# Four early expert units instead of three in a fused two-block transformer kernel on one core

## The chip, the core and the metric

One core of one Trainium2 chip runs the whole program. TensorE (PE), VectorE (DVE), ScalarE (ACT), GpSimd (POOL) and SyncE (SP) run their own instruction streams and meet in semaphores; 16 DMA engines move data between HBM and the on-chip memory. The metric is the device time of one execution in microseconds, the median of several. Before the change that is 3735.68 us (3734.17 to 3736.08, 3 runs).

## The reference

Two transformer blocks on 256 tokens of width 2048, all in float32. The first has two layers of attention with grouped and latent heads, the second one layer of attention beside a linear recurrence. The change lies in the last part, a layer of 16,384 experts, of which each token uses 16 in each of 8 heads:

```python
def _peer(h, w_q, k1, k2, u, vt):
    q = (h @ w_q).reshape(B, S, PEER_HEADS, 2, PEER_HALF)
    s1, s2 = (scores of the two halves of q against 128 keys each)
    v1, i1 = lax.top_k(s1, 16)
    v2, i2 = lax.top_k(s2, 16)
    cand = v1[..., :, None] + v2[..., None, :]          # 256 pairs
    vs, ic = lax.top_k(cand, 16)
    e = (index of the pair) = i1 * 128 + i2
    w = jax.nn.softmax(vs, axis=-1)
    act = jax.nn.gelu(einsum('thkd,td->thk', take(u, e), h)) * w
    return einsum('thk,thkd->td', act, take(vt, e))
```

`u` and `vt` are 16,384 x 2048 each, 134 MB.

## The kernel before

The tokens stand in two tiles of 128. A unit is one head of one token tile, so there are 16 units, units 0 to 7 of the first tile and 8 to 15 of the second. For a unit, every token needs 16 rows of `vt`, and 16 dot products of its activations with rows of `u`. A gathered row is one indirect DMA: each of the 128 partitions (tokens) gets its own row of 2048 floats, 1 MB in all.

The kernel gets the dots in two ways. For most units it computes all of them: the dense stage multiplies the activations with the whole of `u`, 128 panels of 1 MB each (512 experts by 4 parts of the contraction), and stores the dots to HBM after every fourth panel (`act_gemm`, L1096 to L1108). Each panel is loaded by SP into one of four buffers, which is free when the remainders of the panel four before are done (L691 to L697). Float32 products are made of three rounded ones: ACT rounds each half panel (`act_half`, L1056), DVE makes the remainder (`dve_half`, L1069), and PE multiplies the halves, 12 matmuls each (`pe_dense`, L856). There are four half panel buffers, and `paced` (L1041) has DVE and ACT issue halves up to two panels ahead of the step that they are in.

Beside it, within the same stage, the first `EARLY` = 3 units are computed in another way: their rows of `u` and then of `vt` are gathered, 32 a unit, and DVE does with each row one instruction, a product summed into a dot for `u` (L1313) or a scaled row added to the sum for `vt` (L1324). After each panel's work, DVE calls `dve_early` with the panel's number `k_`, and ACT `act_early`. A unit has 42 panels: at step 0 its keys are chosen (`choose_keys`, L1584), at step 1 its experts (`choose_experts`, L1591, which ends in the index that POOL waits for), and then the rows follow on four panels of five. There are three row slots (`EARLY_SLOTS`), and POOL gathers row r when DVE is done with row r - 3 (L773 to L784). In the last of the early units the steps without a row also hold the choice of units 3 and 4, the first late ones.

The late stage (`peer`) has the other `LATE` = 16 - `EARLY` = 13 units. POOL gathers for each 16 columns of stored dots and 16 rows of `vt` into 8 slots (L787 to L819); DVE sums 11 of the rows of a unit (L1642) and PE the other five, with the coefficients on a diagonal (L1012). Units from the third late one on are chosen by DVE within this stage, two units ahead (L1632 to L1635). The coefficients of the next unit are made at the end of each unit (L1623). After the eighth unit and at the end the sums are added to `yacc` (L1648, L1649).

In each engine the instructions run in the order of the program; POOL's queue starts with the early rows, and the late gathers wait until all of the dense stage is done on the three engines (L785).

Of the kernel before, what the change touches and what calls it, by code (L numbers as in the profile page):

```python
# [22 lines left out]
ALU = mybir.AluOpType  # L23
# [23 lines left out]
TOPK = 16  # L47


EARLY = 3  # L50
EARLY_STEPS = 2 * TOPK + 10
EARLY_SLOTS = 3
DENSE_SLOTS = 4
PE_ROWS = (2, 5, 8, 11, 14)
# [53 lines left out]
def build(nc, panels, ada, xin, cvec, cols_d, consts_d, bada_d, bf_d, peer_u, peer_v, out):  # L108
    plan = make_plan()
    ctx = ExitStack()  # L110
    with ctx:
# [3 lines left out]
        def sem(name):  # L115
            return ctx.enter_context(nc.semaphore(name))
# [20 lines left out]
        def region(off, *shape):  # L137
            n = int(np.prod(shape))
            v = memh[:, off:off + n] if off < AR else memr[:, off - AR:off - AR + n]
            if len(shape) == 2:  # L140
                v = v.rearrange("p (a b) -> p a b", a=shape[0])
            if len(shape) == 3:
                v = v.rearrange("p (a b c) -> p a b c", a=shape[0], b=shape[1])
            return v
# [38 lines left out]
        def con(name, w):  # L183
            return consts[:, CONSTS[name]:CONSTS[name] + w]
# [380 lines left out]
        hx = region(AR + 8192, D)  # L565
# [12 lines left out]
        yacc = region(B, 2, D)  # L578
# [132 lines left out]
        NSLOT = 8  # L711
        LATE = 2 * HEADS - EARLY
        rows = region(RING, NSLOT, D)
# [7 lines left out]
        early_rows = region(ADAR, EARLY_SLOTS, D)  # L721
# [10 lines left out]
        def small(*shape, dt=F32):  # L732
            v = region(small_at[0], *shape)
            small_at[0] += int(np.prod(shape))
            return v if dt is F32 else v.bitcast(dt)
# [16 lines left out]
        act16 = small(2, TOPK)  # L752
        gel16 = small(TOPK)
        coef = small(TOPK)
# [4 lines left out]
        early_in = [sem(f"early_in{i}") for i in range(EARLY_SLOTS)]  # L759
        early_used = sem("early_used")  # L760
# [3 lines left out]
        def _(pool):  # L764
# [7 lines left out]
            begin(pool, "pool", early_st)  # L772
            for n in range(EARLY):  # L773
                pool.wait_ge(idx_ready, n + 1)
# [12 lines left out]
            def dot(m, j):  # L787

                if j == 0:
                    pool.wait_ge(idx_ready, EARLY + m + 1)  # L790
                    pool.sem_inc(held, 1)
                pool.indirect_dma_start(
                    out=late_act[:, m, j:j + 1], out_offset=None, in_=dots[:, :],
                    in_offset=bass.IndirectOffsetOnAxis(ap=eidx[:, EARLY + m, j:j + 1], axis=0),
                ).then_inc(dots_in[m % 2], 16)

            def row(m, j):

                r = m * TOPK + j
                if r >= NSLOT:  # L800
# [4 lines left out]
                    out=rows[:, r % NSLOT, :], out_offset=None, in_=peer_v[:, :],  # L805
                    in_offset=bass.IndirectOffsetOnAxis(ap=idx[:, EARLY + m, j:j + 1], axis=0),
                ).then_inc(row_in[r % NSLOT], 16)
# [18 lines left out]
        def one_unit(s_, n):  # L826
            if isinstance(n, int):
                return s_[:, n, :]
            return s_[:, bass.ds(n, 1), :].rearrange("p a b -> p (a b)")
# [172 lines left out]
        def pe_peer(pe, st):  # L1002
            for m in range(LATE):
                t, first = (EARLY + m) // HEADS, m in (0, HEADS - EARLY)
                if first and t:
# [265 lines left out]
        def act_wexp(act, n):  # L1271

            act.wait_ge(vs_ready, n + 1)
            act.activation(vexp[:, :], vs[:, :], ACT.Exp, bias=nvs[:, 0:1], accum_out=nvs[:, 1:2]).then_inc(wexp_ready, 1)

        LATE_KEYS = {EARLY_STEPS * (EARLY - 1) + 6: EARLY, EARLY_STEPS * (EARLY - 1) + 16: EARLY + 1}
        LATE_EXPERTS = {EARLY_STEPS * (EARLY - 1) + 11: EARLY, EARLY_STEPS * (EARLY - 1) + 26: EARLY + 1}

        def early_row(step, first):

            a, b = divmod(step - first, 5)
            return 4 * a + b if 0 <= a < TOPK // 4 and b < 4 else None

        def act_early(act, k_):

            n, step = divmod(k_, EARLY_STEPS)
            if n < EARLY and step == 1:
                act_wexp(act, n)
            if k_ in LATE_EXPERTS:
                act_wexp(act, LATE_EXPERTS[k_])  # L1290
            if n < EARLY and step == 21:
                act.wait_ge(early_used, 2 * TOPK * n + TOPK)
                act.activation(gel16[:, :], act16[:, n % 2, :], ACT.Gelu_apprx_tanh).then_inc(gelu_ready, 1)

        def dve_early(dve, k_, chain):

            n, step = divmod(k_, EARLY_STEPS)
            if n >= EARLY:
                return
            if step == 0:  # L1300
                choose_keys(dve, n, chain)
            if step == 1:
                choose_experts(dve, n, chain)
            if k_ in LATE_KEYS:
                choose_keys(dve, LATE_KEYS[k_], chain)
            if k_ in LATE_EXPERTS:
                choose_experts(dve, LATE_EXPERTS[k_], chain)
            j = early_row(step, 2)
            if j is not None:
                r = 2 * TOPK * n + j  # L1310
                dve.wait_ge(early_in[r % EARLY_SLOTS], 16 * (r // EARLY_SLOTS + 1))
                row = early_rows[:, r % EARLY_SLOTS, :]
                dve.tensor_tensor_reduce(row, row, hx, 1.0, 0.0, ALU.mult, ALU.add,  # L1313
                                         act16[:, n % 2, j:j + 1]).then_inc(early_used, 1)
            j = early_row(step, 22)
            if j == 0:
                dve.wait_ge(gelu_ready, n + 1)
                dve.tensor_tensor(coef[:, :], gel16[:, :], wgt[:, n, :], ALU.mult).then_inc(coef_ready, 1)
                dve.wait_ge(coef_ready, n + 1)
            if j is not None:  # L1320
                r = 2 * TOPK * n + TOPK + j
                dve.wait_ge(early_in[r % EARLY_SLOTS], 16 * (r // EARLY_SLOTS + 1))
                dve.wait_ge(early_used, r)
                dve.scalar_tensor_tensor(yacc[:, 0, :], early_rows[:, r % EARLY_SLOTS, :], coef[:, j:j + 1], yacc[:, 0, :],  # L1324
                                         ALU.mult, ALU.add).then_inc(early_used, 1)

        def act_peer(act, st, chain):
# [256 lines left out]
        def choose_keys(dve, n, link):  # L1584

            dve.tensor_copy(tok[:, :], one_unit(tokens, n))
            link(dve.tensor_copy(s12[:, :, :].rearrange("p a b -> p (a b)"), one_unit(scores, n)))
            for a in range(2):
                link(top16(dve, link, s12[:, a, :], s12b[:, a, :], v16[:, a, :], i16[:, a, :]))

        def choose_experts(dve, n, link):  # L1591

            dve.tensor_copy(i16f[:, :, :], i16[:, :, :])
            link(dve.tensor_tensor(cand[:, :].rearrange("p (a b) -> p a b", a=TOPK),
                                   v16[:, 0, :].unsqueeze(2).broadcast_to([P, TOPK, TOPK]),
                                   v16[:, 1, :].unsqueeze(1).broadcast_to([P, TOPK, TOPK]), ALU.add))
            link(top16(dve, link, cand[:, :], candb[:, :], vs[:, :], ic[:, :]))
            dve.tensor_scalar(nvs[:, 0:1], vs[:, 0:1], -1.0, None, ALU.mult).then_inc(vs_ready, 1)
            dve.tensor_scalar(ab[:, 0, :], ic[:, :], 4, None, ALU.logical_shift_right)
            link(dve.tensor_scalar(ab[:, 1, :], ic[:, :], 15, None, ALU.bitwise_and))  # L1600
            link(dve.tensor_copy(abf[:, :, :], ab[:, :, :]))
            for a, buf in ((0, cand), (1, candb)):
                eq = buf[:, :].rearrange("p (k j) -> p k j", k=TOPK)
                link(dve.tensor_tensor(eq, abf[:, a, :].unsqueeze(2).broadcast_to([P, TOPK, TOPK]),
                                       con("iota", TOPK).unsqueeze(1).broadcast_to([P, TOPK, TOPK]), ALU.is_equal))
                link(dve.tensor_tensor(eq, eq, i16f[:, a, :].unsqueeze(1).broadcast_to([P, TOPK, TOPK]), ALU.mult))
                link(dve.reduce_sum(e16[:, a, :], eq, AX_X))
            link(dve.scalar_tensor_tensor(abf[:, 0, :], e16[:, 0, :], float(N_KEYS), e16[:, 1, :], ALU.mult, ALU.add))
            dve.tensor_copy(idx[:, n, :], abf[:, 0, :])
            link(dve.tensor_scalar(abf[:, 1, :], abf[:, 0, :], tok[:, :], None, ALU.add))  # L1610
            dve.tensor_copy(eidx[:, n, :], abf[:, 1, :]).then_inc(idx_ready, 1)
            dve.wait_ge(wexp_ready, n + 1)
            link(dve.reciprocal(nvs[:, 2:3], nvs[:, 1:2]))
            dve.tensor_scalar(wgt[:, n, :], vexp[:, :], nvs[:, 2:3], None, ALU.mult)
# [183 lines left out]
```

## Time and profile before

| | |
|---|---|
| median of 3 runs | 3735.68 us |
| profiled execution | 3738.8 us |
| its span | 3737.1 us |
| mean granted clock of PE | 0.91 |
| busy share of the span: PE, DVE, ACT, POOL | 84%, 67%, 31%, 16% |
| moved by DMA | 915.92 MB, mean 245 GB/s |

Busy times of PE are modelled from pipelined matmuls, so that a matmul of the dense stage has a record of some 390 ns while the next starts before its end. The time of a stage is therefore read from the starts and from the windows, and not from the sum of durations. The share of DMA in a window is the mean busy share of the 16 DMA engines; the granted clock is the part of 2.4 GHz that PE was given.

### The profile page before, as it was taken

The page shows a single profiled execution, that of the slowest core. Times are in us where ns is not written, and L with a number is a line of the kernel's source. Part 1 is how long each engine was busy: PE and PEld are TensorE (multiplying, and loading weights), DVE is VectorE, ACT ScalarE, POOL GpSimd, SP SyncE. Part 2 cuts the span into 40 slices and gives each one's busy share as a digit, 9 for nine tenths or more (in the row PEclk, how much of TensorE's full clock was granted, in tenths as well). Part 3 has the DMA queues.
Part 4 walks back from the last instruction along what each step waited for, and adds up shares of the span by engine and source line. Part 5 has one row for each costly group of instructions (what it writes and reads, how often), then busy time and mean ns, then how long its engine had stood idle before and what let it go on. Part 6 is the DMA issues. An engine that isn't in the chain of part 4 may idle for free.

```text
span 3737.1 us, 39190 instructions
## 1 busy us (share of the span) xinstructions
PE 3130.6 (84%) x14772; PEld 2358.0 (63%) x14772; DVE 2504.1 (67%) x3403; ACT 1153.2 (31%) x1749; POOL 597.4 (16%) x692
## 2 busy tenths in 40 slices
PE   6699998988979989997999689999999984545555
PEld 1488875446758886486997589787887861112222
DVE  4988876746776656455562554777777855778775
ACT  1421225133242343244442443344443430111101
POOL 0000000000100000000000000111111126666662
PEclk9899999989979999898996799999999997777777
DMA  8555760524866763354651234898997968889996
GB/s 350 211 217 226 267 259 1 185 86 181 314 236 249 284 221 124 146 200 168 219 182 38 108 137 175 323 371 309 384 367 309 355 264 302 349 345 361 357 362 262
DMA packets 146983, 915.92 MB, mean 245 GB/s; under 512 B 21617, under 2 KB 30065, under 8 KB 40433
## 3 DMA queue, kind: packets, MB, share of 16 engines
q0 software_dynamic: 75776, 503.47, 35.4%
q1 hardware_dynamic: 56912, 384.82, 26.8%
q10 hardware_dynamic: 14112, 25.17, 1.8%
q8 instruction: 118, 1.93, 0.2%
q14 instruction: 65, 0.52, 0.0%
HBM read 884.03 MB, written 29.36 MB: 244 GB/s over the span
## 4 chain that ended last, share of the span: by engine, by line
PE 60%; DVE 20%; DMA 6%; PEld 5%; issue 4%; ACT 2%; another core or an unknown queue 1%; POOL 0%; DVEq 0%; SPq 0%; ACTq 0%; PEldq 0%; POOLq 0%
PE psum L896 29%; PE psum L869 17%; DVE psum L1642 7%; PEld psum L896 5%; PE psum L973 5%; PE psum L903 5%; DVE junk L1380 2%; PE psum L990 2%; DMA memr<-in_ada_dram 2%; DMA memr<-in_peer_v_dram,memr 2%; DMA memr<-in_panels_dram 1%; PE psum L981 1%; DVE w_lo L1073 1%; PE psum L914 1%
## 5 line engine op out<-in xcount | busy, mean ns | idle before, releaser
L1073 DVE TENSOR_TENSOR w_lo<-memr,w_hi 128x1024 fp32r<-128x1024 f32 x614 | 740.0, 1222 | 457.9 <-ACT w_hi L1067 456.7
L1067 ACT ACTIVATE w_hi<-memr 128x1024 fp32r<-128x1024 f32 x614 | 641.8, 1056 | 954.9 <-PE psum L896 317.4
L1380 DVE CUSTOM_DVE_ANT_0 junk<-memr 128x2048 bf16<-128x2048 f32 x256 | 585.7, 2288 | 126.5 <-DMA memr<-in_ada_dram 85.5
L896 PE MATMUL psum<-h_hi,w_hi 128*128 128x512 f32 (+1 forms) x1696 | 602.4, 355 | 70.0 <-DVE h_lo L1451 47.8
L896 PE MATMUL psum<-h_lo,w_hi 128*128 128x512 f32 (+1 forms) x1696 | 590.3, 348 | 0.0
L896 PE MATMUL psum<-h_hi,w_lo 128*128 128x512 f32 (+1 forms) x1696 | 590.3, 348 | 0.0
L1012 PE MATMUL psum<-memr,memh 128*128 128x512 f32 x520 | 323.3, 780 | 311.3 <-DMA memr<-in_peer_v_dram,memr 198.1
L1012 PEld LDWEIGHTS psum<-memr,memh 128*128 128x128 f32 x520 | 126.0, 254 | 508.2 <-issue 428.6
L869 PE MATMUL psum<-w_hi,l_hi 128*128 128x512 f32 x1024 | 403.5, 394 | 28.6 <-DVE w_lo L1073 28.6
L869 PE MATMUL psum<-w_hi,l_lo 128*128 128x512 f32 x1024 | 402.2, 393 | 0.0
L896 PEld LDWEIGHTS psum<-h_hi,w_hi 128*128 128x128 f32 x1696 | 325.4, 192 | 121.4 <-issue 66.8
L869 PE MATMUL psum<-w_lo,l_hi 128*128 128x512 f32 x1024 | 401.8, 392 | 0.0
L896 PE MATMUL psum<-l_hi,w_hi 128*128 128x256 f32 x1168 | 342.6, 293 | 31.3 <-DVE l_lo L1451 20.9
L771 POOL DMA_DIRECT2D memr<-in_ada_dram x174 | 91.9, 528 | 1717.0 <-DVE mod L1383 1709.7
L1642 DVE SCALAR_TENSOR_TENSOR psum<-memr,memh,psum 128x2048 f32<-128x2048 f32 x141 | 332.0, 2355 | 42.6 <-DMA memr<-in_peer_v_dram,memr 28.0
L896 PEld LDWEIGHTS psum<-h_lo,w_hi 128*128 128x128 f32 x1696 | 326.3, 192 | 41.5 <-issue 3.1
L896 PEld LDWEIGHTS psum<-h_hi,w_lo 128*128 128x128 f32 x1696 | 325.9, 192 | 39.5
L896 PE MATMUL psum<-l_lo,w_hi 128*128 128x256 f32 x1168 | 336.4, 288 | 0.0
L896 PE MATMUL psum<-l_hi,w_lo 128*128 128x256 f32 x1168 | 336.2, 288 | 0.0
L896 PEld LDWEIGHTS psum<-l_hi,w_hi 128*128 128x128 f32 x1168 | 229.8, 197 | 37.4 <-issue 31.8
L869 PEld LDWEIGHTS psum<-w_hi,l_hi 128*128 128x128 f32 x1024 | 194.6, 190 | 72.4 <-DVE w_lo L1073 25.5
L896 PEld LDWEIGHTS psum<-l_lo,w_hi 128*128 128x128 f32 x1168 | 230.7, 198 | 0.4
(182 smaller groups left out, 3816.2 us busy)
## 6 DMA issues: line engine op xcount, KB each, us to landing
memr<-in_panels_dram SPq DMA_DIRECT2D x339, 1024.0 KB, 6.4
memr<-in_ada_dram POOLq DMA_DIRECT2D x176, 1024.0 KB, 5.9
dots<-sq ACTq DMA_DIRECT2D x64, 256.0 KB
memr<-in_xin_dram SPq DMA_DIRECT2D x1, 4096.0 KB, 14.1
gstore<-sq ACTq DMA_DIRECT2D x16, 256.0 KB
memh<-gstore SPq DMA_DIRECT2D x2, 2048.0 KB, 8.0
memr<-gstore SPq DMA_DIRECT2D x2, 2048.0 KB, 10.1
memr<-in_xin_dram SPq DMA_DIRECT2D x2, 2048.0 KB, 7.3
```

Source lines behind the costliest of these rows:

```text
L771: pool.dma_start(adar[:, s_, :], ada[i * 2 + s_]).then_inc(ada_in[s_], 16)
L869: ins = pe.matmul(bank(2 * (group % 2) + t), x_[:, kc, t * P:t * P + P], u_[:, c, :], start=kc == 0 and j == 0, stop=kc == DC - 1 and j == 2)
L896: ins = pe.matmul(bank(o["bank"])[:, 0:o["w"]], w_[:, c, :], x_[:, kc, :], start=kc == 0 and j == 0, stop=kc == DC - 1 and j == 2)
L903: ins = pe.matmul(bank(o["bank"])[:, a:b], lt, rh, start=j == 0, stop=j == len(pairs) - 1)
L914: pe.matmul(bank(4 + gr["ms"] % 2)[:, 0:w], ones[:, :], sq[:, n % 2, 0:w], start=j == 0, stop=j == len(gr["x"]) - 1).then_inc(sq_used, 1)
L973: ins = pe.matmul(o, lt, rh, start=j == 0, stop=j == len(mms) - 1, skip_group_check="forget" in u)
L990: ins = pe.matmul(bank(O_BANK + u["hn"] % 2)[:, u["col"]:u["col"] + P], u["v"][c], probT[:, u["n"] % 2, c * P:c * P + P], start=c == 0, st ...
L1012: ins = pe.matmul(bank(b), diags[:, q % DIAGS, :], rows[:, r % NSLOT, 512 * b:512 * b + 512], start=first and i == 0, stop=(EARLY + m) % H ...
L1067: act.activation(w_hi[:, m % HALVES, :, :], slot[:, 8 * i:8 * i + 8, :], ACT.Copy).then_inc(hi_ready, 1)
L1073: dve.tensor_tensor(w_lo[:, m % HALVES, :, :], raw_panel(o["g"])[0][:, 8 * i:8 * i + 8, :], w_hi[:, m % HALVES, :, :].bitcast(F32), ALU.su ...
L1380: chain(dve.tensor_tensor_reduce(junk[:, :], w, cact[:, v_, :], 1.0, 0.0, ALU.mult, ALU.add, mod[:, a, m:m + 1]))
L1642: dve.scalar_tensor_tensor(sums_dve, row, by, sums_dve, ALU.mult, ALU.add).then_inc(row_added, 1)
```

## The change

`EARLY` goes from 3 to 4, and the steps of an early unit from 42 to 32, so that the four units take the 128 panels exactly. Every panel now has a row: step j handles row j of `u` for j < 16 and row j - 16 of `vt` after. Keys and experts of unit 0 are chosen together at the first panel; those of unit n + 1 are chosen at steps 8 and 20 of unit n, beside its rows. The second late unit is chosen at panels 118 and 124. The gelu of a unit moves from step 21 to step 15, and its coefficients to step 16. `LATE` becomes 12, by its definition.

```diff
-EARLY = 3
-EARLY_STEPS = 2 * TOPK + 10
+EARLY = 4
+EARLY_STEPS = 2 * TOPK
...
-        LATE_KEYS = {EARLY_STEPS * (EARLY - 1) + 6: EARLY, EARLY_STEPS * (EARLY - 1) + 16: EARLY + 1}
-        LATE_EXPERTS = {EARLY_STEPS * (EARLY - 1) + 11: EARLY, EARLY_STEPS * (EARLY - 1) + 26: EARLY + 1}
-
-        def early_row(step, first):
-
-            a, b = divmod(step - first, 5)
-            return 4 * a + b if 0 <= a < TOPK // 4 and b < 4 else None
+        KEYS_AT = {EARLY_STEPS * n + 8: n + 1 for n in range(EARLY)}
+        EXPERTS_AT = {EARLY_STEPS * n + 20: n + 1 for n in range(EARLY)}
+        KEYS_AT[EARLY_STEPS * EARLY - 10], EXPERTS_AT[EARLY_STEPS * EARLY - 4] = EARLY + 1, EARLY + 1
...
-            if n < EARLY and step == 1:
-                act_wexp(act, n)
-            if k_ in LATE_EXPERTS:
-                act_wexp(act, LATE_EXPERTS[k_])
-            if n < EARLY and step == 21:
+            if k_ == 0:
+                act_wexp(act, 0)
+            if k_ in EXPERTS_AT:
+                act_wexp(act, EXPERTS_AT[k_])
+            if step == TOPK - 1:
                 act.wait_ge(early_used, 2 * TOPK * n + TOPK)
                 act.activation(gel16[:, :], act16[:, n % 2, :], ACT.Gelu_apprx_tanh).then_inc(gelu_ready, 1)
...
-            if step == 0:
-                choose_keys(dve, n, chain)
-            if step == 1:
-                choose_experts(dve, n, chain)
...
+            if k_ == 0:
+                choose_keys(dve, 0, chain)
+                choose_experts(dve, 0, chain)
+            if k_ in KEYS_AT:
+                choose_keys(dve, KEYS_AT[k_], chain)
+            if k_ in EXPERTS_AT:
+                choose_experts(dve, EXPERTS_AT[k_], chain)
+            r = 2 * TOPK * n + step
+            row = early_rows[:, r % EARLY_SLOTS, :]
+            if step == TOPK:
                 dve.wait_ge(gelu_ready, n + 1)
                 dve.tensor_tensor(coef[:, :], gel16[:, :], wgt[:, n, :], ALU.mult).then_inc(coef_ready, 1)
                 dve.wait_ge(coef_ready, n + 1)
...
+            dve.wait_ge(early_in[r % EARLY_SLOTS], 16 * (r // EARLY_SLOTS + 1))
+            if step < TOPK:
+                dve.tensor_tensor_reduce(row, row, hx, 1.0, 0.0, ALU.mult, ALU.add,
+                                         act16[:, n % 2, step:step + 1]).then_inc(early_used, 1)
+            else:
+                j = step - TOPK
                 dve.wait_ge(early_used, r)
-                dve.scalar_tensor_tensor(yacc[:, 0, :], early_rows[:, r % EARLY_SLOTS, :], coef[:, j:j + 1], yacc[:, 0, :],
+                dve.scalar_tensor_tensor(yacc[:, 0, :], row, coef[:, j:j + 1], yacc[:, 0, :],
                                          ALU.mult, ALU.add).then_inc(early_used, 1)
```

## Rows read from the trace of the kernel before

**Rows 1.** Windows by stretch: us, busy (count) of PE, PEld, DVE, ACT, POOL; clock; DMA share; GB/s.
```profile
2334.00:3068.00 734.00, 708.49 (x3072) 582.83 (x3072) 567.75 (x624) 307.63 (x336) 111.17 (x96) 0.98 0.87 339
...
3104.00:3347.50 243.50, 126.11 (x200) 49.27 (x200) 184.69 (x282) 26.59 (x56) 153.89 (x164) 0.76 0.87 333
3347.50:3702.00 354.50, 197.22 (x320) 76.71 (x320) 268.06 (x360) 29.01 (x65) 214.47 (x227) 0.77 0.92 364
```

**Rows 2.** The same view, an undisturbed piece of the dense stage.
```profile
2380.00:2560.00 180.00, 180.00 (x796) 149.10 (x795) 137.20 (x108) 79.33 (x84) 28.32 (x26) 1.00 0.96 374
```

**Rows 3.** Timeline of DVE, two row steps: start us, us, instruction.
```profile
2402.18 2.29 DVE L1313 CUSTOM_DVE_ANT_0 memr<-memr 128x2048 f32<-128x2048 f32 x1
...
2407.62 2.29 DVE L1313 CUSTOM_DVE_ANT_0 memr<-memr 128x2048 f32<-128x2048 f32 x1
```

**Rows 4.** Chain of waits in the dense stage: start us, us, what.
```profile
2370.12 209.26 PE psum L869 x912
...
2608.44 206.81 PE psum L869 x900
...
2847.42 40.87 PE psum L869 x168
```

**Rows 5.** Windows at the second unit start and at a late choice of experts.
```profile
2590.00:2620.00 30.00, 22.98 (x90) 18.11 (x89) 22.49 (x37) 9.92 (x13) 6.67 (x6) 0.89 0.82 320
...
2890.00:2920.00 30.00, 29.63 (x131) 24.21 (x130) 28.28 (x49) 13.89 (x17) 5.00 (x4) 1.00 0.89 341
```

**Rows 6.** Timeline of DVE in the late stage: the coefficients of four units.
```profile
3143.16 0.17 DVE L1623 TENSOR_TENSOR memh<-memh,memr 128x16 f32<-128x16 f32 x1
3195.54 0.17 DVE L1623 TENSOR_TENSOR memh<-memh,memr 128x16 f32<-128x16 f32 x1
...
3623.75 0.17 DVE L1623 TENSOR_TENSOR memh<-memh,memr 128x16 f32<-128x16 f32 x1
3662.20 0.17 DVE L1623 TENSOR_TENSOR memh<-memh,memr 128x16 f32<-128x16 f32 x1
```

**Rows 7.** Timeline of DVE at the first unit start.
```profile
2343.44 0.15 DVE L1586 COPY memr<-consts 128x1 f32<-128x1 f32 x1
...
2348.13 2.36 DVE L1073 TENSOR_TENSOR w_lo<-memr,w_hi 128x1024 fp32r<-128x1024 f32 x2
...
2357.62 0.17 DVE L1611 CAST memr<-memr 128x16 uint32<-128x16 f32 x1
...
2357.90 0.23 DVE L1614 TENSOR_SCALAR memr<-memr 128x16 f32<-128x16 f32 x1
...
2366.63 2.29 DVE L1313 CUSTOM_DVE_ANT_0 memr<-memr 128x2048 f32<-128x2048 f32 x1 [6.24 <-DMA memr<-in_peer_u_dram,memr]
```

**Rows 8.** DMA issues of the last 1737 us, with KB each and us to landing.
```profile
memr<-in_panels_dram SPq DMA_DIRECT2D x160, 1024.0 KB, 5.0
dots<-sq ACTq DMA_DIRECT2D x64, 256.0 KB
```

**Rows 9.** Windows in which the DMA engines were busy all the time or nearly.
```profile
2840.00:2870.00 30.00, 25.03 (x100) 20.12 (x99) 23.51 (x36) 9.95 (x12) 4.57 (x4) 0.89 1.00 410
2990.00:3020.00 30.00, 30.00 (x134) 24.84 (x133) 25.47 (x18) 12.65 (x13) 9.09 (x5) 1.00 1.01 409
3650.00:3680.00 30.00, 18.39 (x30) 7.00 (x28) 19.09 (x10) 1.78 (x6) 13.70 (x15) 0.77 1.01 419
2600.00:2700.00 100.00, 94.88 (x408) 77.99 (x407) 75.17 (x66) 39.98 (x42) 16.13 (x16) 0.97 0.98 384
```

**Rows 10.** The early gathers on POOL (L781): issue duration ns min/median/max, and landing.
```profile
L781 POOL DMA_INDIRECT memr<-in_peer_u_dram,memr x48: 932/1140/1577, 2358.8 to 2929.3; - x48
...
DMA to landing us min/median/max: 5.6/9.8/12.8
```

**Rows 11.** The page's group of ACT's roundings: busy, mean ns, idle before.
```profile
L1067 ACT ACTIVATE w_hi<-memr 128x1024 fp32r<-128x1024 f32 x614 | 641.8, 1056 | 954.9 <-PE psum L896 317.4
```

**Rows 12.** Waits in the dense stage: engine line waited for: us in total, times, longest.
```profile
DVE memr L1313 <- DMA memr<-in_peer_u_dram,memr: 18.7, 3, 6.3
```

## What the change was forecast to do, worked out from these rows

> **What bounds the kernel now.** I read the stretches first [rows 1]: dense dots 2334 to 3068 us, a fill, the sums of late units 3104 to 3702 us, and an end of 35 us. Dense and late stretch have different limits, and that is the whole question, since the change carries work from the second to the first.
>
> In the dense stretch 3072 matmuls (128 panels of 24) keep PE busy; an undisturbed piece has 796 of them in 180 us [rows 2], so 24 x 180 / 796 = 5.43, and the row steps of DVE come 5.44 us apart [rows 3]. 128 x 5.44 = 696 us, while the window that holds all 3072 is 734.0 long [rows 1], some 3 us of it at its edges (the matmuls end at about 3066.5): 34 us are lost. The chain of waits shows where [rows 4]: PE runs undisturbed from 2370.1 to 2579.4 and from 2608.4 to 2815.3; at each of the three unit starts DVE chooses a unit and then stands for its first gathered row [the first in rows 7], and PE runs dry behind it. The second start has 7.0 us of PE idle in 30 and a granted clock of 0.89, so part ran at 1.2 and not 2.4 GHz [rows 5]. From 2370.12 to 2608.44 are 84 half panels, 228.5 us of work in 238.3: one such start costs 9.8 us, the next (to 2847.42) 10.5.
>
> In the late stretch DMA is what is short: share 0.87 and 0.92, PE busy about half, DVE about three quarters [rows 1]. The coefficients of consecutive units stand at 3143.16 and, ten units later, 3623.75 [rows 6]: 48.06 us a unit for 16 rows.
>
> **The change, part by part. Base:** the profiled execution took 3738.8 us (span 3737.1); the runs' median is 3735.68, 3.1 less. Differences are worked out in the profile and set on the median.
>
> (1) A late unit goes: 13 to 12. Units 4 and 5 are now chosen beforehand, as 3 and 4 were, and the last two need no choice either, so the missing one is a middle one, with its choice: **-48.1 us**. Bounds: the last units' spacing of 38.5 (3623.75 to 3662.20) and the first's 52.4. The fill and the end stay.
>
> (2) Two unit starts in the dense stage go, units 1 and 2, since each choice now comes while the unit before is still being gathered: -9.8 - 10.5 = **-20.3**. The row that was late there is then asked for as any other row is. What is late next is (4) and (5).
>
> (3) The first start gets worse. Now four half panels of DVE work stand between keys, experts and the first row; after the change none do. The choice ran from 2343.44 to 2358.1 with one pair of remainders (2.3) from 2348.13 on in it [rows 7]: keys 4.7, experts 7.7. Without the pair it ends at 2355.8; the row is there 8.8 us after its index (2357.8 to 2366.6), which now stands at 2355.5, so 2364.3, its product ends 2366.6 and the next half panel's remainder 2367.8. PE starts half 5 then, where before it started half 9 at 2370.12. Four halves are 10.9 us, less 2.2 gained: **+8.7**. Bounds 5 and 12, by when the first four rows come. The one slow-clock piece stays.
>
> (4) Choices beside rows. In steady work DVE finishes a half panel 2.3 us after PE frees its buffer (ACT's rounding 1.06 [rows 11], the remainder 1.2), and PE isn't out of halves until 4 x 2.72 = 10.9 us after. With a row (2.3) and the next remainder (1.2) DVE is done at 5.8: 5.1 us of cover. Keys (4.7) fit. Experts (7.7) miss by 2.6, in four places. Before, a late choice of experts stood on a step without a row, with 5.1 + 2.3 = 7.4 us of cover, and cost 0.37 us of PE (29.63 busy of 30 [rows 5]) where this reckoning gives 0.3. DVE then catches up at 5.44 - 2.3 - 2.35 = 0.8 us a panel, enough for the 12 to 20 panels to the next choice. The last pair (experts at 116, keys 118, experts 124) doesn't get that time: about 3 us each. Sum 4 x 2.6 + 6 - 0.7 = +15.7. The gelu after row 15 makes ACT wait for DVE's product and load a table, some 2.7 us, inside the cover. Bounds: 0 if panels are late anyway, +13 more if each stall costs slow clock as a start does.
>
> (5) Bytes. A panel and a row are 1.049 MB each, the dots stored 0.131 MB a panel [rows 8]. Before, 4 of 5 panels had a row: 10.09 MB in 27.2 us = 371 GB/s wanted, and 374 at a share of 0.96 was moved [rows 2]. After: 2.228 MB in 5.44 us = 410 GB/s wanted. What can be had? Thirty-microsecond pieces at a share of 1.00 or 1.01 moved 410 and 409 GB/s in this stage and 419 in the late one; 100 us at 0.98 moved 384, so 392 full [rows 9]. I take 397: 5.61 us a panel, 0.17 over PE's, x 118 panels = +20. DMA thus becomes the limit, barely. It works on while DVE chooses (up to three rows and four panels are on order), so of (4) only some 4 us come on top: (4) and (5) together **+24**. Bounds: 16 (410 holds, PE's own rate), and 60 at 377 GB/s.
>
> Total bytes give much the same: when the first row is issued (2356.5) 122 panels, 128 rows and 16.8 MB of dots are left, 278.9 MB / 397 = 702 us, to 3059; in the last four panels nothing but rows is left to load, 9 us unused, and five choices let the queues run thin by 1 or 2 us each: end at about 3077 against 3066.5, +11. The parts give -20.3 + 8.7 + 24 = +12.4.
>
> (6) Rows 126 and 127 are now summed beside the last panels, DVE done before PE's last half and the last dots are stored; +1 for that tail (0 to 5).
>
> Sum: -48.1 + 12.4 + 1 = -34.7, rounded -35: **3701 us** (3704 for a profiled execution).
>
> Where page and trace differ: a full share gives 392 to 419 GB/s here [rows 9]. The Trainium skill, DMA: Bandwidth & Descriptors, "Where 436 GB/s comes from", says of HBM to SBUF that the HBM side binds, at about 358; an estimate by that page is 285.2 MB (278.9 and the six panels before) / 358 = 797 us of dense stage, 66 more than now, and a total some 18 us slower. The trace speaks against it in this run. The same skill's HBM Reference, "Specifications", names it the share when both cores of a pair stream, and about 425 for one alone.
>
> **Rivals.**
>
> A, DMA keeps up at 410 and (5) is nothing: dense -20.3 + 8.7 + 15.7 = +4, total -43: 3693. For it: 409 and 410 over 30 us. Against: 392 full over 100 us.
>
> B, each wait costs more than itself: DVE has 4.65 of 5.6 us filled, and a late row holds up the next remainders and so PE, with the clock behind it. Say 384 GB/s, the best 100 us [rows 9]: 5.80 us, +0.36 x 118 = 42, and 4: dense +34, total -13: 3723. For it: the tight coupling of one DVE stream with both gates. Against: now DVE waits for a row three times only, 18.7 us in all, the three starts [rows 12].
>
> C, slower: three row slots are too few once there is no panel without a row. A slot's round is the sum (2.35), 0.3 until POOL has it, the issue 1.14 and the landing, shared by three: with the median landing of 9.8 us [rows 10] 4.5 us a row, with the longest, 12.8, 5.5. The spare panels that let the slots refill are gone. With a landing of 15 us a row takes 6.26: 0.82 x 118 = 97, dense +85, total +38: 3774. It costs more than it saves from 5.91 us a panel on (118 x 0.47 = 56, with 4 the 60 above), a landing of 13.9 us. For it: landings must grow as the share stays at 1. Against: growth stops when the rows on order fall. By the Trainium skill (DMA: Bandwidth & Descriptors, "Queues, rings and completion order") each DMA engine takes turns between queues that have work; by that, panels couldn't starve the rows. No row shows the sharing itself.
>
> D, the memory side gives no more over a whole stage than the 364 GB/s that the long late piece moved [rows 1]: (278.9 + 6.3) MB / 364 = 784 us, +53 in dense, total +5: 3741. Against: that piece had a share of 0.92, so it wasn't full. By the page's 358, above, this is what would happen.
>
> **How the numbers follow.** Forecast 0.49, A 0.20, B 0.18, C 0.10, D 0.03. A measurement of this kernel tells 0.2% (7.5 us) from no change. Faster: forecast and A, and four fifths of B, 0.83; same 0.06, from B's slow end and the mild end of C; slower 0.11. Range for 8 in 10: from 3680 (A with (3) and (4) near their low ends) to 3738 (377 to 384 GB/s).
>
> **What would show it.** Dense stage: DMA share at 1.00 in nearly all windows, 392 to 405 GB/s, 5.6 us between row steps, matmuls ending about 741 us after their start; one start stall of some 18 us and no others of that kind; DVE waits for rows in the middle of units. Late stage: 12 x 16 rows, the same 48 us a unit, the same 36 us fill. Wrong if DMA's share there stays at 0.97 with panels at 5.44 (A), if row landings pass 13 us with the share under 0.95 (C), or if late units take other than 45 to 50 us.

## The result and the profile after

The changed kernel takes 3704.12 us (3702.0 to 3706.42, 4 runs) against 3735.88 for the kernel before beside it; ratio 0.991, 95% interval 0.9891 to 0.9928. The forecast was 3701, faster. The total came out as forecast; two of its terms, (4) and (5), did not, and nearly cancelled, so that the total is right in part by luck.

The changed kernel's windows, as in [rows 1]: dense stage, then the late units of the first and of the second tile.

```profile
2342.00:3087.00 745.00, 714.16 (x3070) 586.43 (x3071) 647.34 (x716) 308.64 (x338) 141.90 (x128) 0.97 0.93 378
...
3122.00:3316.00 194.00, 97.69 (x160) 38.36 (x160) 144.41 (x226) 20.54 (x43) 122.50 (x131) 0.77 0.86 327
3316.00:3670.00 354.00, 198.58 (x320) 76.88 (x320) 272.14 (x361) 31.82 (x71) 217.69 (x231) 0.79 0.94 370
```

Where each stage begins and ends is read best from the first and last start of one instruction: PE's third product of the dense stage (L869), the coefficients of a late unit (L1613) and the closing sums (L1638). Durations are min/median/max in ns, then the starts in us.

```profile
L869 PE MATMUL psum<-w_lo,l_hi x1024: 387/389/628, 2344.3 to 3087.4; 128*128 128x512 f32 x171
...
L1613 DVE TENSOR_TENSOR memh<-memh,memr x12: 168/169/231, 3125.3 to 3626.4; 128x16 f32<-128x16 f32 x12
...
L1638 DVE TENSOR_TENSOR memh<-psum,memh x2: 2291/2292/2292, 3315.9 to 3670.5; 128x2048 f32<-128x2048 f32 x2
```

The same three instructions in the kernel before:

```profile
L869 PE MATMUL psum<-w_lo,l_hi x1024: 387/389/628, 2336.8 to 3066.0; 128*128 128x512 f32 x171
...
L1623 DVE TENSOR_TENSOR memh<-memh,memr x13: 167/168/176, 3103.8 to 3662.2; 128x16 f32<-128x16 f32 x13
...
L1648 DVE TENSOR_TENSOR memh<-psum,memh x2: 2291/2292/2292, 3342.9 to 3702.1; 128x2048 f32<-128x2048 f32 x2
```

So, in the two profiled executions (spans 3737.1 and 3704.5):

| | before | after | |
|---|---|---|---|
| up to the dense stage | 2336.8 | 2344.3 | +7.5 |
| dense matmuls | 729.2 | 743.1 | +13.9 |
| fill | 37.8 | 37.9 | +0.1 |
| late units | 598.3 (13) | 545.2 (12) | -53.1 |
| end | 35.0 | 34.0 | -1.0 |
| span | | | -32.6 |

The first line is no work of the change: nothing ahead of the dense stage differs, and over the twelve profiles of this study that start lies anywhere from 2332.7 to 2354.8 (three of them clear the sums later, which is worth 3.5).

The line of the late units holds something that the change didn't do, too. The unit that goes is one of the first token tile. Up to the first closing sums that tile's late units took 239.1 us before (3103.8 to 3342.9) and 190.6 after (3125.3 to 3315.9): 48.5 less. The other 4.6 us came in the eight units of the second tile, on which nothing was changed: 359.2 before, 354.6 after, and 360.9 when the changed kernel ran again (e0).

Windows of 30 us in the changed kernel's dense stage: two that PE fills, and two with a choice of experts in them.

```profile
2740.00:2770.00 30.00, 30.00 (x134) 24.86 (x133) 24.30 (x22) 13.63 (x15) 6.44 (x6) 1.00 1.01 406
2800.00:2830.00 30.00, 30.00 (x134) 24.86 (x133) 26.12 (x22) 14.04 (x15) 6.63 (x6) 1.00 1.02 425
...
2470.00:2500.00 30.00, 26.98 (x113) 21.88 (x112) 28.26 (x41) 11.90 (x15) 6.16 (x5) 0.94 0.91 361
3010.00:3040.00 30.00, 26.98 (x106) 21.71 (x106) 27.46 (x56) 11.50 (x15) 4.63 (x4) 0.89 0.87 355
```

DMA moves up to 425 GB/s with a row on every panel, and PE has no idle there: it isn't held to 397. The time goes in the other windows, 3.0 us of PE idle each. The chain of waits has PE's pieces behind the first start and behind four of the five choices of experts, and the timeline of PE has its wait at the first of these choices.

```profile
2372.91 46.51 PE psum L869 x192
...
2488.04 97.04 PE psum L869 x420
...
2667.40 97.14 PE psum L869 x420
...
2846.97 98.40 PE psum L869 x420
...
3027.97 33.11 PE psum L869 x132
```

```profile
2488.04 0.80 PE L869 MATMUL psum<-w_hi,l_hi 128*128 128x512 f32 x1 [3.02 <-DVE w_lo L1073]
```

192 matmuls are 16 half panels, 43.5 us of work, and took 3.0 more. 420 are 35 halves, 95.2 us, and took 1.8, 1.9 and 3.2 more; 132 are 11 halves, 29.9 us, and took 3.2 more: the slow clock behind the idle time (granted 0.94 in the window of the first choice, 0.89 in that of the fourth). PE's idle time was 3.0 to 3.1 us at each of the five; behind the fifth, three halves before the end of the stage, 1.9 more went to the slow clock. A choice of experts thus costs 4.8 to 6.3 us.

Waits of the changed kernel in the dense stage (us in total, times, longest; 6.5 us of the first line lie ahead of the stage's first matmul):

```profile
PE psum L869 <- DVE w_lo L1073: 35.8, 8, 13.5
...
DVE memr L1309 <- DMA memr<-in_peer_u_dram,memr: 17.0, 13, 6.2
...
DVE memh L1314 <- DMA memr<-in_peer_v_dram,memr: 4.3, 8, 1.0
```

DVE now waits for rows in the middle of units, 21 times instead of 3 [rows 12], but for 21.3 us in all, 6.2 of them at the start.

### The profile page after: what moved, and what is told of

Same layout as the page of the kernel before. It is cut to its first block, busy times and chain, and to the rows that moved or that the text cites. A ratio compares the mean times of both kernels' runs of the same rounds, so it can differ in the third digit from the quotient of the medians.

```text
span 3704.5 us, 39156 instructions
## 1 busy us (share of the span) xinstructions
PE 3104.6 (84%) x14732; PEld 2344.8 (63%) x14732; DVE 2548.1 (69%) x3440; ACT 1150.6 (31%) x1744; POOL 597.9 (16%) x692
## 4 chain that ended last, share of the span: by engine, by line
PE 58%; DVE 19%; DMA 7%; issue 5%; PEld 5%; POOL 3%; ACT 2%; another core or an unknown queue 1%; DVEq 0%; ACTq 0%; SPq 0%; PEldq 0%; POOLq 0%
PE psum L896 28%; PE psum L869 15%; PEld psum L896 5%; DVE psum L1632 5%; PE psum L973 5%; PE psum L903 5%; DMA memr<-in_ada_dram 3%; DVE junk L1370 3%; PE psum L990 2%; DVE w_lo L1073 2%; DMA memr<-in_peer_v_dram,memr 1%; POOL memr L804 1%; PE psum L981 1%; POOL memh L792 1%; DMA memr<-in_panels_dram 1%
## 5 line engine op out<-in xcount | busy, mean ns | idle before, releaser
L1012 PE MATMUL psum<-memr,memh 128*128 128x512 f32 x480 | 296.3, 776 | 285.4 <-DMA memr<-in_peer_v_dram,memr 181.1
L869 PE MATMUL psum<-w_hi,l_hi 128*128 128x512 f32 x1024 | 406.6, 397 | 36.0 <-DVE w_lo L1073 35.8
L1012 PEld LDWEIGHTS psum<-memr,memh 128*128 128x128 f32 x480 | 115.2, 252 | 466.0 <-issue 423.1
L869 PE MATMUL psum<-w_hi,l_lo 128*128 128x512 f32 x1024 | 404.3, 395 | 0.0
L869 PE MATMUL psum<-w_lo,l_hi 128*128 128x512 f32 x1024 | 403.7, 394 | 0.0
L1632 DVE SCALAR_TENSOR_TENSOR psum<-memr,memh,psum 128x2048 f32<-128x2048 f32 x130 | 306.1, 2355 | 62.7 <-DMA memr<-in_peer_v_dram,memr 37.9
L869 PEld LDWEIGHTS psum<-w_hi,l_hi 128*128 128x128 f32 x1024 | 195.8, 191 | 81.5 <-DVE w_lo L1073 33.9
```

Of the source, the lines that this page charges most:

```text
L869: ins = pe.matmul(bank(2 * (group % 2) + t), x_[:, kc, t * P:t * P + P], u_[:, c, :], start=kc == 0 and j == 0, stop=kc == DC - 1 and j == 2)
L1012: ins = pe.matmul(bank(b), diags[:, q % DIAGS, :], rows[:, r % NSLOT, 512 * b:512 * b + 512], start=first and i == 0, stop=(EARLY + m) % H ...
L1632: dve.scalar_tensor_tensor(sums_dve, row, by, sums_dve, ALU.mult, ALU.add).then_inc(row_added, 1)
```

## The experiments

Three groups of kernels ran, each beside its own runs of the kernel before: e1, e2, e3 and e5; then e0, e4 and e6; then e7, e8 and e9. The medians of the kernel before were 3685.67, 3747.0 and 3739.35 us. Totals are therefore differences of medians within a group; the ratios are worked out from all runs and need not be those of the medians. Stage times are from one profiled execution each, dense matmuls as in the table above.

| kernel | total against before, ratio (95%) | dense | late (units) |
|---|---|---|---|
| e1, overlap alone | -23.4, 0.9936 (0.992 to 0.9953) | 710.4 | 537.5 (13) |
| e2, cut choices | -55.5, 0.9852 (0.9836 to 0.9869) | 718.3 | 494.5 (12) |
| e3, two slots | +57.6, 1.0154 (1.0134 to 1.0174) | 838.9 | 494.4 (12) |
| e5, soft start | -72.5, 0.9802 (0.9786 to 0.9818) | 704.7 | 492.2 (12) |
| e0, the change again | -34.0, 0.9903 (0.9871 to 0.9935) | 743.1 | 545.9 (12) |
| e4, five early | +8.9, 1.0016 (0.9995 to 1.0037) | 840.0 | 503.2 (11) |
| e6, e5 with half panels | -88.3, 0.9751 (0.9713 to 0.9789) | 700.4 | 547.5 (12) |
| e8, the change with half panels | -30.7, 0.9919 (0.9887 to 0.995) | 742.7 | 548.5 (12) |
| e7, e4 with half panels | -44.4, 0.9878 (0.9842 to 0.9915) | 780.2 | 494.8 (11) |
| e9, e5 again | -77.5, 0.9795 (0.9756 to 0.9833) | 706.7 | 548.1 (12) |

**Overlap alone (e1).** Three early units with the rows where they were; the choices of units 1 and 2 move to rowless panels of the unit before. Against the kernel before (panel: unit; both pieces of a choice of experts stand on one panel, so that it isn't cut):

```diff
-            if step == 0:
-                choose_keys(dve, n, chain)
-            if step == 1:
-                choose_experts(dve, n, chain)
...
+        KEYS_AT = {0: 0, 26: 1, 68: 2, 90: 3, 100: 4}
+        PICK_AT = {1: 0, 31: 1, 73: 2, 95: 3, 110: 4}
+        EXPERTS_AT = {1: 0, 31: 1, 73: 2, 95: 3, 110: 4}
```

> One part of the change alone: still three early units on 126 panels and a row on four panels of five, but units 1 and 2 are chosen on rowless panels while the unit before is summed. Theory 1 (step 2 of the forecast: a unit start costs 10 us of the dense stage because its first row is asked for too late): dense matmuls take 730.6 - 20 = 710 us, the late stage stays at 598, total 3716 us. Rival (the starts cost nothing of their own, the lost time is DVE work that has to be done anyway): 730 us and 3736.

Dense 710.4 us:

```profile
L868 PE MATMUL psum<-w_lo,l_hi x1024: 388/389/632, 2334.9 to 3045.3; 128*128 128x512 f32 x171
```

18.8 less than in the profile before, and 23.4 of the total (20 expected). The profile before belongs to another group, but dense stages repeat across groups: 743.1 twice for the changed kernel, 704.7 and 706.7 for e5 and e9. Step (2) stands: a start cost the wait for its row, and that is gone when the row is asked for early.

**Cut choices (e2).** `choose_experts` becomes `pick_pairs` (to the 16 best pairs) and `name_experts` (the rest), on different panels. The keys move too, and the last choices move apart.

```diff
-        KEYS_AT = {EARLY_STEPS * n + 8: n + 1 for n in range(EARLY)}
-        EXPERTS_AT = {EARLY_STEPS * n + 20: n + 1 for n in range(EARLY)}
...
+        KEYS_AT = {0: 0, 4: 1, 36: 2, 68: 3, 98: 4, 113: 5}
+        PICK_AT = {0: 0, 11: 1, 43: 2, 75: 3, 103: 4, 118: 5}
+        EXPERTS_AT = {0: 0, 19: 1, 51: 2, 83: 3, 108: 4, 123: 5}
```

> The changed kernel, with the choice of experts cut in two (the top 16 pairs, 3.5 us; the naming of the experts, 4.2 us) on panels some seven apart, so that no piece of choosing is over the 5.1 us of cover. Theory 1 (DMA can carry 410 GB/s; what the changed kernel loses in the dense stage are five stalls of PE behind an uncut choice of 7.7 us, some 3 us of idle and 1.8 us of slow clock each): dense matmuls 744 - 24 = 720 us, total 3680 us. Theory 2 (step 5 of the forecast: DMA's 397 GB/s sets 5.61 us a panel whatever DVE does): at least 738 us, total 3698 or more.

Windows of e2: the whole stage, and two of 30 us at the places where the changed kernel had a choice of experts.

```profile
2341.00:3060.00 719.00, 703.25 (x3072) 578.97 (x3070) 644.10 (x715) 309.27 (x338) 148.02 (x128) 0.99 0.96 391
2470.00:2500.00 30.00, 30.00 (x133) 24.54 (x132) 29.02 (x32) 14.90 (x19) 5.89 (x5) 1.00 1.01 402
2650.00:2680.00 30.00, 30.00 (x134) 24.86 (x133) 28.80 (x20) 12.74 (x14) 7.31 (x6) 1.00 1.00 398
```

718.3 us, 24.8 under the changed kernel, with the same bytes and the same DVE work. Theory 1 holds to 2 us, and in the total as well (-55.5, where 3680 meant -56); theory 2 would have kept the stage over 738. The cover of 5.1 us, worked out in step (4), the time that DVE can be away beside a row before PE runs dry, is the size that matters: behind the start, PE waits three times in this stage, 0.5, 1.1 and 0.4 us, where it waited 3.0 to 3.1 five times. How much the new places of the last choices add to the cut isn't separated; the first four uncut choices had 12 panels without a choice before them, and cost PE as much idle time as the fifth.

**Two row slots (e3).** `EARLY_SLOTS = 2` in the changed kernel.

> The changed kernel with two row slots instead of three. Rival C's reckoning, a slot's round shared by the slots: (2.35 + 0.3 + 1.14 + 9.8) / 2 = 6.8 us a row with the landing of before, dense 870 to 890 us, total 3840; if the landing falls to some 7.8 us with fewer rows on order, 5.8 us a row, dense 762 us, total 3722. If slots don't matter at all: 3704.

```profile
L869 PE MATMUL psum<-w_lo,l_hi x1024: 387/389/632, 2335.0 to 3173.9; 128*128 128x512 f32 x171
...
DMA to landing us min/median/max: 5.7/9.1/12.5
```

```profile
DVE memr L1309 <- DMA memr<-in_peer_u_dram,memr: 98.1, 54, 6.4
DVE memh L1314 <- DMA memr<-in_peer_v_dram,memr: 70.4, 45, 5.8
```

Rival C's round gives (2.35 + 0.3 + 1.14 + 9.1) / 2 = 6.45 us a row with the landing measured, 825 us for 128 rows; 838.9 were measured. That is 2% off, with a landing known only afterwards. The stage is 31 to 51 us shorter than the 870 to 890 that I expected, since the landing came down from 9.8 to 9.1 (0.35 us a row, 45 us); the total of 3840 meant +104, and +57.6 came. C's mechanism is real, DVE waiting 168 us for rows in 99 waits; three slots are just clear of it: in e2 the median landing is 11.9 us and the round (3.8 + 11.9) / 3 = 5.2, under the 5.44 of a panel.

**Soft start (e5, and again as e9).** On top of e2: first choice in three pieces on panels 0, 1 and 2, clearing on panel 3, row r on panel r + 4, and four panels with two rows.

```diff
+        KEYS_AT = {0: 0, 12: 1, 40: 2, 66: 3, 92: 4, 108: 5}
+        PICK_AT = {1: 0, 21: 1, 47: 2, 73: 3, 98: 4, 115: 5}
+        EXPERTS_AT = {2: 0, 28: 1, 54: 2, 79: 3, 104: 4, 121: 5}
+        ROWS_AT = lambda k_: tuple(range(k_ - 4 + sum(k_ > d for d in (34, 61, 87, 126)), k_ - 3 + sum(k_ >= d for d in (34, 61, 87, 126)))) if k_ >= 4 else ()
...
+            if k_ == 3:
+                chain(dve.memset(yacc, 0.0))
...
-            if st.get("early"):
-                chain(dve.memset(yacc, 0.0))
```

> The kernel with the cut choices, and a start in which DVE makes its remainders between the pieces of the first choice, clears the sums on panel 3 instead of ahead of the stage, and takes the first row on panel 4; the four rows that are then behind are taken as a second row on panels 34, 61, 87 and 126. Theory 1: the start's 19 us (16 idle, 3 slow clock) fall to under 4, and 3.5 us of clearing go from ahead of the first matmul: dense matmuls 705 us, total 3662 us. Rival (two rows on one panel, or the end of the stage with two rows to sum, give it back): 3672 or more.

704.7 us, as expected (705). Within the stage PE waits 1.3 us at the longest, where it waited 13.5, and 3.5 us ahead of its first matmul, where that was 6.5.

```profile
2340.00:3045.00 705.00, 699.54 (x3071) 575.22 (x3071) 644.95 (x716) 311.11 (x340) 149.14 (x128) 1.00 0.98 401
3104.00:3500.00 396.00, 231.70 (x377) 89.67 (x376) 351.42 (x534) 46.23 (x99) 292.49 (x310) 0.81 1.01 403
```

> The kernel with the cut choices and the soft start once more, beside others of this group, to see whether its 72.5 us hold where the kernel before is slower than it was beside it the first time. The dense stage gives 730.6 - 704.7 + 3.5 = 29 us on any chip; a late unit fewer gave between 43 and 53 us. So 72 to 82 us, ratio 0.978 to 0.981.

-77.5 us and 0.9795, as expected, dense 706.7. It is the best kernel of the study.

```profile
3104.00:3500.00 396.00, 211.53 (x331) 82.22 (x332) 309.31 (x461) 41.08 (x87) 256.86 (x272) 0.78 0.91 356
```

This last row is e9's late stage, to be held against e5's above: the same program, 403 GB/s at a share of 1.01 in one, 356 at 0.91 in the other. The late units took 492.2 and 548.1 us, 55.9 apart, where the kernel before differs by 53.7 between the two groups.

**The change again (e0).**

> The changed kernel as it is, beside the others of this group. If the stalls behind the uncut choices are its loss, its dense matmuls again take 743 to 745 us, and it stands 24 us over the kernel with the cut choices. If it takes 5 us less or more, the 24 us can't be put down to them.

743.1, which is 24.8 over e2, and 34.0 us less than before: the first result repeats.

**Five early units (e4).** e2 with `EARLY = 5`, row r on panel 4r/5, seven choices.

> The kernel with the cut choices and one step further: five early units, five rows on four panels, 11 late units, seven choices in the dense stage. Theory 1 with a DMA ceiling at the 412 GB/s that its 60 us windows showed at a share of 1.00: 318.9 MB / 412 = 774 us and the start, dense matmuls 780 to 790, 65 more than with four, late stage 45 to 50 less, so 15 to 20 us slower than with four cut choices, 35 to 40 under the kernel before. Rival, no ceiling that near and only DVE's own work counts (292 us of remainders, 360 of rows, 86 of choices, 740 with the coefficients): dense 750 to 755, and 15 us faster than with four.

Both were wrong: 840.0 us, and no gain over the kernel before. (The profiled execution took 3771.8, 15.8 over the median of the ten runs and the largest such distance here, so that a usual one may have a stage some 15 us shorter.) Waits, then the window over its dense stage:

```profile
PE psum L868 <- DVE w_lo L1072: 101.2, 38, 17.0
DVE memr L1307 <- DMA memr<-in_peer_u_dram,memr: 42.5, 25, 6.2
DVE memh L1312 <- DMA memr<-in_peer_v_dram,memr: 37.2, 24, 3.2
```

```profile
2354.00:3195.00 841.00, 746.22 (x3072) 599.90 (x3072) 724.84 (x808) 311.33 (x343) 214.53 (x160) 0.94 0.94 374
```

No engine is full there: DVE 725 of 841 us, DMA share 0.94. DVE stands 80 us for rows, PE 95 us for DVE (and 6.5 ahead of the stage), and PE's clock is at 0.94.

**Half panels (e6, e8, e7).** One edit in three kernels. It leaves out the loads of half of each panel, so that the dots of those experts are not the right ones; the work of PE, DVE and ACT is the same:

```diff
-                sp.dma_start(region(dense_at[s_], PANEL), panels[i]).then_inc(u_in[s_], 16)
+                sp.dma_start(region(dense_at[s_], PANEL)[:, 0:PANEL // 2], panels[i][:, 0:PANEL // 2]).then_inc(u_in[s_], 16)
```

> The changed kernel with half of the columns of each panel of u not loaded (their dots are computed from what is there); DVE's, ACT's and PE's work is as it was. Step 5 of the forecast (DMA is the limit of the changed kernel's dense stage and costs 20 us): dense matmuls 743 - 20 = 723 us. Theory 1 (the stage loses 48 us to the start and to uncut choices, none to bytes): 740 to 744 us.

```profile
2342.00:3087.00 745.00, 714.16 (x3072) 586.36 (x3072) 645.61 (x716) 308.78 (x339) 142.56 (x128) 0.97 0.81 290
```

290 instead of 378 GB/s, and PE's busy time and the stage's length are the same to 0.4 us (742.7). DVE's waits for rows went with the bytes, from 21.3 us in 21 times to three times, 6.5 us of them at the start:

```profile
DVE memr L1309 <- DMA memr<-in_peer_u_dram,memr: 7.7, 3, 6.5
```

So PE felt neither the bytes nor the waits for rows in the middle of units; step (5) is refuted by its own test.

> The kernel with the cut choices and the soft start, with half of the columns of each panel of u not loaded (the dots of those are computed from what is there), so that 313 instead of 409 GB/s are wanted. Theory: there DMA was just at its limit and took some 9 us from the 695.6 us that 128 panels need (704.7 measured); with half panels 697 to 700 us, the waits for rows gone (36 us in 39 times before). Rival: those 9 us are DVE's choices and double rows, and stay: 703 to 705 us.

700.4 against 704.7: 4 us go with the bytes, where I had given them 9. The same program twice, e5 and e9, lies 2 us apart, so that the 4 are hardly clear of what one program varies by.

> The kernel with five early units (dense matmuls 840 us), with half of the columns of each panel not loaded: 360 instead of 458 GB/s wanted at PE's own pace. If its loss comes from bytes (a ceiling on DMA, and waits for rows that PE feels through DVE): 750 to 765 us. If it is DVE's own work that doesn't fit (740 us of it, and pieces of choosing that come before the cover is back): over 810 us.

780.2: between my two cases. Of the 144 us by which e4's stage is over PE's own 696, 60 go with the bytes; the other 84 stay. I take them for DVE's work, which leaves too little time to catch up between choices (the half-panel kernel has DVE busy 721 of 781 us), but no run separates that.

## Why the forecast held, step by step

(1) A middle unit less, -48.1 forecast, -53.1 measured, inside its bounds. The first tile, from which the unit went, gave 48.5, as forecast; the other 4.6 are the spread of the second tile's units between executions. How much a unit is worth goes with the group and the execution: 43.0 in the first group (537.5 and 494.5), 42.7 in the second (545.9 and 503.2), 53.7 in the third (548.5 and 494.8). These are single profiles, and what moves the price isn't shown.

(2) -20.3, measured alone 18.8 (e1). Right.

(3) +8.7 forecast. PE began at 2343.34 with five halves, 13.6 us of work, and went on at 2372.91: 16.0 us lost, of which 13.5 were idle and the rest went to the slow clock of the stage's first matmuls (until 2347.7 they start 0.43 us apart, then 0.23). Behind the wait 3.0 more went to the slow clock. Before, PE began at 2335.86 with nine halves and went on at 2370.12, 9.8 us lost, and 2.5 behind it [rows 4]. So +6.7. Right.

(4) and (5), +24 together, are mis-sized apart and by luck nearly right together. (4) was put at 15.7 and counted for only 4 of it, since DMA was to be the limit anyway. In truth the stage, 744.3 us from its first matmul to the end of its last, lost 744.3 - 696 = 48 us, less 19 for the start: 29 for ten choices. The idle time was sized right: 16.4 forecast (15.7 after 0.7 was taken off for the choices of before), and 15.3 at the five choices of experts and 0.4 at one of keys measured. What I had left in the bounds, 13 us of slow clock, came: 12.0, between 1.8 and 3.2 a choice. That makes 27.7 of the 29. Of (5)'s 20 us nothing came (e8).

The step that failed is the ceiling. I took 397 GB/s, between the 409 and 410 that windows at full share had moved in this stage and the 392 of 384 / 0.98 [rows 9]. That division takes the share for the part of a ceiling that is used, which the kernel before already spoke against. It asked for 371 GB/s in the mean, and where PE was never idle it had a share of 1.00 at 388:

```profile
2620.00:2650.00 30.00, 30.00 (x134) 24.85 (x133) 22.76 (x21) 13.35 (x16) 4.16 (x4) 1.00 1.00 388
```

The windows at a share of 1.00 to 1.02 that are shown above moved 406 and 425, and one of e2 398: the share didn't say how much more could be had.

(6) is within what can't be told apart.

The rivals: A had the mechanism (DMA keeps up) and, with the slow clock of (4) in it, would have given some 3705; I gave it 0.20. B and C were not it at three slots and 409 GB/s. C's round sets the pace with two slots (e3). B's mechanism shows with five units, where 60 us go with the bytes (e4 and e7). D falls: 401 GB/s over 705 us in e5. So does the sum by the page behind it, the 358 GB/s of the Trainium skill's DMA: Bandwidth & Descriptors, "Where 436 GB/s comes from". The Trainium skill's HBM Reference, "Specifications", has about 425 for a core that streams alone, and the window of 425 agrees; e5's 401 over the whole stage, with about 409 asked for, doesn't go against it.

## What to carry to other kernels

A long in-order piece on an engine that feeds another is free up to the cover of the buffers between them, and beyond it costs idle time and clock; cutting it in two at the same work took off 25 us here. Before a busy share is read as a ceiling, take bytes away: one run with half the loads settled what the share of four rows couldn't. Work moved beside a bound engine is cheap until the spare time of its helpers is gone: the fourth unit cost the dense stage 14 us, and the fifth 122 over the kernel with the cut choices (in the profiled execution; some 16 less by the median of its runs), for the 43 to 54 that each saves later.

## What the runs showed of the hardware

The same program's late stage, gathers alone, ran at 403 GB/s and a share of 1.01 in one group and 356 at 0.91 in another (e5, e9), while its dense stage took the same time within 2 us. The kernel before took 3685.67 us in the first group and 50 to 61 more beside the others and beside the change. By the record's numbers the first and third group ran on the same chip, 5, and the second on chip 10, so which chip it was doesn't explain it. What makes the difference stays open.

3.0 to 3.1 us of idle in a stream of matmuls were followed by a loss of 1.8 to 3.2 us to the lower clock (1.2 instead of 2.4 GHz), 5.1 us in the kernel before (with 1.9 us of idle shortly ahead of them) by 2.5 and 2.8, and 13.5 us by only 3.0. In e5, with no idle over 1.3 us in the stage, the granted clock was 1.00.
